# Attention probabilities of the wide units: the transposed unit leaves PSUM through two engines, one bank each

## The chip, the cores and the metric

One NeuronCore of a Trainium2 chip runs the whole kernel. The metric is the device time of one execution in microseconds, the median of three runs; lower is better.

## The reference

A decoder trunk of two layers over 256 tokens of width 1024, in float32. Only the attention matters here:

```python
# layer 0: for each of 8 heads, the selected-block and the window branch of one
# attention, and a top-k branch (dsa) of another; layer 1: 16 heads of "fox"
s = q @ k.T * HEAD_DIM ** -0.5 (+ bias)     # causal
p = softmax(where(valid, s, -1e30))
o = p @ v
...
x = layer_norm(ALPHA * x + concat(o) @ w_o)
x = layer_norm(ALPHA * x + moe(x))          # 64 experts, top 8, plus a shared one
```

## The kernel before

Each engine has an instruction stream of its own, written out by hand, and semaphores order them. Layer 0 projects the inputs, runs the attention, the output projection (`wo`), a layer norm, the router and the shared expert, and then 32 steps of two experts each. Layer 1 does the same with another attention. SyncE issues the weight loads into a ring of four slots, each load when the matmuls that read the slot's old contents are done.

**The attention pipeline.** The work is cut into units of four heads by 128 queries. Layer 0 has 12 units and layer 1 has 8. In the first half of each list (t = 0: units 0 to 5, and 0 to 3) a head has 128 keys, in the second half (t = 1: units 6 to 11, and 4 to 7) it has 256. A unit of t = 1 is called wide: its transposed probabilities are 128x1024 and fill PSUM banks 4 and 5; those of a t = 0 unit are 128x512 and fill bank 4. All engines run over the same iterations u, and in iteration u

- TensorE: the scores of unit u (L598, in layer 1 also L602) and its mask (L614) into PSUM banks 0 to 3; then the transposes of unit u-3 (L634) into banks 4 and 5; then the product with the values (L668, in layer 1 L663) of unit u-4. When there are no scores left, iterations 12 to 15 (8 to 11 in layer 1) have eight matmuls of `wo` (L703) behind the rest.
- VectorE (DVE): the row maxima of unit u (L1523), the copy of unit u-3 from PSUM into `pT` (L1533, one instruction over both banks), then the coefficients of unit u-1 (L1545, L1550) and the scaling of its last head (L1555). Now and then it copies a finished output bank into `xT` (L1560).
- ScalarE (ACT): four exponentials with row sums of unit u (L1214), now and then an output bank into `xT` (L1228).
- GpSimd (POOL): scales three heads of unit u-1 (L531) once its coefficients are there.

Each engine executes its stream in order. There is one pair of banks for the transposes, so TensorE waits before the transposes of unit v for the copy of unit v-1:

```python
pe.wait_ge(sem("sc_scaled"), B + v + 1)
pe.wait_ge(sem("sc_scaled_last"), B + v + 1)
if v:
    pe.wait_ge(sem("pT_copied"), B + v)
```

`B` is 0 in layer 0 and 12 in layer 1. `UNITS` is the list of units, each (kind, t, g); `pT` has two halves, for even and odd units. `PIECE` is 512, one bank.

Of the kernel before, what the change touches and what calls it, by code (L numbers as in the profile page):

```python
# [7 lines left out]
ACT = mybir.ActivationFunctionType  # L8
# [48 lines left out]
PIECE = 512  # L57
# [52 lines left out]
def build_trunk(nc, a, out):  # L110
    with ExitStack() as ctx:
# [253 lines left out]
        def n_keys(t):  # L365
            return (t + 1) * P

        def unit_slots(g):

            return [4 * g + 2 * j + parity for parity in range(2) for j in range(2)]  # L370
# [181 lines left out]
        def _(pe):  # L552
# [22 lines left out]
            def attention(L):  # L575
# [3 lines left out]
                for u in range(U + 4):  # L579
                    if L == 0 and u == 2:  # L580

                        pe.wait_ge(sem("roped"), 5)
                        transpose_pairs(5)
                    if L == 0 and u == 3:
                        pe.wait_ge(sem("qkT_copied"), 6)
                    if u < U:
                        what, t, g = units[u]
                        K = n_keys(t)
                        if u >= 2:

                            pe.wait_ge(sem("sc_exp"), B + u - 1)
                        for j in range(2):

                            heads = [(unit_slots(g)[2 * half + j], slice(HD * half, HD * half + HD),
                                      ps[:, 2 * (u % 2) + half, j * K:(j + 1) * K]) for half in range(2)]
                            for h, r, o in heads:
                                q0, k0, _ = BRANCH.get(what, (0, 2 * 8 + 2 * (h // 2), None))
                                ins = pe.matmul(o, qkT[r, (q0 + h) // 2 if what != "fox" else h // 2, t * P:(t + 1) * P],  # L598
                                                qkT[r, k0 // 2, 0:K], start=j == 0, stop=False, skip_group_check=True)
                            if what == "fox":  # L600
                                for h, r, o in heads:
                                    ins = pe.matmul(o, aug_q[r, h // 2, t * P:(t + 1) * P], aug_k[r, 0:K],  # L602
                                                    start=False, stop=False, skip_group_check=True)
                        if u == 0 and L == 0:
                            pe.wait_ge(sem("causal_cast"), 1)
                        if what == "dsa":
                            pe.wait_ge(sem("selected"), t + 1)
                        for half in range(2):
                            o = ps[:, 2 * (u % 2) + half, 0:2 * K].rearrange("p (s k) -> p s k", s=2)
                            if what == "dsa":  # L610
                                mask, n = selected_bf[t], K
                            else:
                                mask, n = causal_bf, P
                            ins = pe.matmul(o[:, :, K - n:K], ident_bf, mask.unsqueeze(1).to_broadcast([P, 2, n]),  # L614
                                            start=False, stop=True, skip_group_check=True)
                        ins.then_inc(sem("sc_mm"), 1)
                    if L == 0 and u == 2:

                        pe.wait_ge(sem("cmp_p"), NT)
                        for tt in range(NT):  # L620
                            ins = pe.transpose(ps[:, 6, tt * P:(tt + 1) * P], cmp_s[:, tt, :], ident)
                        ins.then_inc(sem("cmp_pT"), 1)
                    if 3 <= u < U + 3:
                        v = u - 3
                        t = units[v][1]

                        pe.wait_ge(sem("sc_scaled"), B + v + 1)
                        pe.wait_ge(sem("sc_scaled_last"), B + v + 1)
                        if v:
                            pe.wait_ge(sem("pT_copied"), B + v)  # L630
                        for s in range(4):
                            for c in range(t + 1):
                                b = s * (t + 1) + c
                                ins = pe.transpose(ps[:, 4 + b // 4, (b % 4) * P:(b % 4 + 1) * P],  # L634
                                                   scores[:, v % 4, s * n_keys(t) + c * P:s * n_keys(t) + (c + 1) * P],
                                                   ident)
                        ins.then_inc(sem("unit_tp"), 1)
                    if L == 0 and u in CMP_STEP:

                        tt = CMP_STEP.index(u)  # L640
                        pe.wait_ge(sem("cmp_pT_copied"), 1)
                        for j in range(4):
                            pe.matmul(ps[:, 7, j * P:(j + 1) * P], v_bd[:, j * P:(j + 1) * P], small_pT[:, tt, :],
                                      start=False, stop=False, skip_group_check=True)
                    if u >= 4:
                        v = u - 4
                        what, t, g = units[v]
                        bank = out_bank(what, g)
                        pe.wait_ge(sem("pT_copied"), B + v + 1)
                        if t and (bank, t) not in opened:  # L650

                            n = [e[0:2] for e in OUTS[L]].index((bank, 0))
                            pe.wait_ge(sem("oT_act" if n % 2 == 0 else "oT_dve"), 2 * L + n // 2 + 1)
                        probs = pT[:, v % 2, 0:4 * (t + 1) * P].rearrange("p (s c k) -> p s c k", s=4, c=t + 1)
                        first = (bank, t) not in opened
                        opened.add((bank, t))
                        c0 = (2 * g % 4) * P
                        for c in range(t + 1):
                            if what == "fox":
                                for j in range(2):  # L660
                                    for half in range(2):
                                        h = unit_slots(g)[2 * half + j]
                                        ins = pe.matmul(ps[half * HD:(half + 1) * HD, bank, c0 + j * P:c0 + (j + 1) * P],  # L663
                                                        v_fox[:, c, h * HD:(h + 1) * HD], probs[:, 2 * half + j, c, :],
                                                        start=first and c == 0 and j == 0, stop=c == t, skip_group_check=True)
                            else:
                                for half in range(2):
                                    ins = pe.matmul(ps[half * HD:(half + 1) * HD, bank, c0:c0 + 2 * P],  # L668
                                                    proj[:, c, BRANCH[what][2]:BRANCH[what][2] + HD],
                                                    probs[:, 2 * half:2 * half + 2, c, :],  # L670
                                                    start=first and c == 0, stop=c == t, skip_group_check=True)
                        ins.then_inc(sem("pv_mm"), 1)
                    if u >= U:

                        i = u - U
                        if i == 0:
                            pe.wait_ge(sem("oT_act"), 2 * L + 1)
                            pe.wait_ge(sem("oT_dve"), 2 * L + 1)
                            pe.wait_ge(sem("sc_exp"), B + U)
                        wo(L, 0, i // 2, range(4 * (i % 2), 4 * (i % 2) + 4))  # L680
# [508 lines left out]
        def _(act):  # L1189
# [12 lines left out]
            def attention(L):  # L1202
                units = UNITS[L % 2]
                U, B = len(units), FIRST_UNIT[L]
                for u in range(U + 4):
                    if u < U:
# [6 lines left out]
                        for s in range(4):  # L1213
# [2 lines left out]
                                                 ACT.Exp, bias=neg_max[:, u % 2, s:s + 1],  # L1216
                                                 accum_out=denom[:, u % 8, s:s + 1])
                        ins.then_inc(sem("sc_exp"), 1)
                    if L == 0 and u == 1:
                        copy_pairs(5, SCALE)  # L1220
                    if L == 0 and u == 2:
# [242 lines left out]
        def _(dve):  # L1464
# [48 lines left out]
            def attention(L):  # L1513
                units = UNITS[L % 2]
                U, B = len(units), FIRST_UNIT[L]
                for u in range(U + 4):
# [9 lines left out]
                    if 3 <= u < U + 3:  # L1526
                        v = u - 3
                        dve.wait_ge(sem("unit_tp"), B + v + 1)
                        if v >= 2:

                            dve.wait_ge(sem("pv_mm"), B + v - 1)
                        n = 4 * n_keys(units[v][1])
                        dve.tensor_copy(pT[:, v % 2, 0:n], ps[:, 4:6, :].rearrange("p b n -> p (b n)")[:, 0:n])\  # L1533
                           .then_inc(sem("pT_copied"), 1)
                    if L == 0 and u == 0:
                        cmp_probs()
                    if 1 <= u <= U:
# [422 lines left out]
```

## Time and profile before

| | |
|---|---|
| median of 3 runs | 1404.83 us (1401.96 to 1406.74) |
| the profiled execution, its own time | 1406.07 us |
| its span, first to last instruction | 1403.8 us |
| mean granted TensorE clock | 0.993 of full speed |
| attention of layer 0 | about 88 to 142 us of the span |
| experts of layer 0 | about 188 to 662 us |
| attention of layer 1 | about 797 to 842 us |
| experts of layer 1 | about 884 to 1362 us |

The times in the rows below are microseconds from the start of the span; 2.3 us of the profiled execution lie outside it. A row of a timeline has the start, the duration, the engine, the line and the operation with its output and input, and in brackets how long the engine stood idle before it and what ended that.

### The profile page before, as it was taken

The page shows a single profiled execution, that of the slowest core. Times are in us where ns is not written, and L with a number is a line of the kernel's source. Part 1 is how long each engine was busy: PE and PEld are TensorE (multiplying, and loading weights), DVE is VectorE, ACT ScalarE, POOL GpSimd, SP SyncE. Part 2 cuts the span into 40 slices and gives each one's busy share as a digit, 9 for nine tenths or more (in the row PEclk, how much of TensorE's full clock was granted, in tenths as well). Part 3 has the DMA queues.
Part 4 walks back from the last instruction along what each step waited for, and adds up shares of the span by engine and source line. Part 5 has one row for each costly group of instructions (what it writes and reads, how often), then busy time and mean ns, then how long its engine had stood idle before and what let it go on. Part 6 is the DMA issues. An engine that isn't in the chain of part 4 may idle for free.

```text
span 1403.8 us, 21736 instructions
## 1 busy us (share of the span) xinstructions
PE 1377.4 (98%) x8662; PEld 848.6 (60%) x8662; DVE 509.4 (36%) x825; ACT 340.0 (24%) x870; POOL 118.3 (8%) x155
## 2 busy tenths in 40 slices
PE   9989999999999999999999999999999999999998
PEld 4555666666566566665488467666656656666553
DVE  1565642332333323234501246232323323333354
ACT  1233232222222222222210222322222222222212
POOL 1555210000000000000100133000000000000000
PEclk9979999999999999999999999999999999999999
DMA  9720459999999999999564504699999999999981
GB/s 303 285 91 1 180 209 411 422 421 420 421 421 420 421 420 421 420 420 383 174 235 149 212 0 180 267 421 421 421 420 421 421 421 421 421 421 420 420 346 60
DMA packets 81110, 461.88 MB, mean 329 GB/s; under 512 B 9216, under 2 KB 9440, under 8 KB 30848
## 3 DMA queue, kind: packets, MB, share of 16 engines
q1 hardware_dynamic: 78432, 452.07, 79.2%
q0 software_dynamic: 2592, 8.53, 2.0%
q8 instruction: 71, 1.16, 0.3%
q14 instruction: 15, 0.12, 0.0%
HBM read 459.52 MB, written 1.05 MB: 328 GB/s over the span
## 4 chain that ended last, share of the span: by engine, by line
PE 88%; DVE 5%; DMA 4%; POOL 1%; issue 1%; ACT 1%; SPq 0%; DVEq 0%; POOLq 0%
PE ps L1025 30%; PE ps L1053 15%; PE ps L1071 9%; PE ps L988 8%; PE ps L703 4%; PE ps L1183 4%; DMA ring<-in_exp_w_dram 3%; PE ps L884 3%; PE ps L805 2%; PE ps L901 2%; PE ps L1035 1%; PE ps L869 1%; PE ps L723 1%; PE ps L598 1%; PE ps L634 1%
## 5 line engine op out<-in xcount | busy, mean ns | idle before, releaser
L1053 PE MATMUL ps<-ring,qkT 128*64 128x512 f32 x1024 | 233.8, 598 | 0.0
L1025 PE MATMUL ps<-ring,proj 128*64 128x256 f32 x2048 | 227.0, 379 | 2.2 <-DMA ring<-in_exp_w_dram 2.2
L1025 PEld LDWEIGHTS ps<-ring,proj 128*64 128x64 f32 x2048 | 147.6, 137 | 88.6 <-issue 20.2
L1822 DVE TENSOR_TENSOR o_tok<-ps,o_tok 128x1024 f32<-128x1024 f32 x124 | 151.8, 1224 | 90.9 <-PE ps L1071 89.9
L1828 DVE TENSOR_TENSOR y_lo<-ps,y_hi 128x1024 fp32r<-128x1024 f32 x62 | 76.0, 1225 | 226.7 <-ACT y_hi L1393 226.7
L1814 DVE SCALAR_TENSOR_TENSOR roped<-roped,rows,ps 128x256 f32<-128x256 f32 x64 | 30.7, 480 | 307.2 <-ACT roped L1366 299.3
L1053 PEld LDWEIGHTS ps<-ring,qkT 128*64 128x64 f32 x1024 | 67.8, 136 | 111.8 <-issue 110.4
L1025 PE MATMUL ps<-ring,pT 128*64 128x256 f32 x1024 | 121.5, 379 | 0.0
L1025 PE MATMUL ps<-ring,gb_row 128*64 128x256 f32 x1024 | 121.4, 379 | 0.0
L1393 ACT ACTIVATE y_hi<-ps 128x1024 fp32r<-128x1024 f32 x62 | 63.5, 1024 | 216.0 <-PE ps L1053 216.0
L1071 PE MATMUL ps<-y_hi,selT 128*128 128x512 f32 x248 | 109.2, 440 | 0.0
L1025 PEld LDWEIGHTS ps<-ring,pT 128*64 128x64 f32 x1024 | 73.4, 137 | 49.5 <-issue 17.1
L1366 ACT ACTIVATE roped<-ps 128x256 f32<-128x256 f32 x64 | 24.6, 385 | 319.1 <-PE ps L1025 319.1
L988 PE MATMUL ps<-sel,x_hi 128*128 128x512 f32 x256 | 101.6, 397 | 0.0
L988 PE MATMUL ps<-sel,x_lo 128*128 128x512 f32 x256 | 100.7, 394 | 0.0
L1071 PE MATMUL ps<-y_lo,selT 128*128 128x512 f32 x248 | 98.5, 397 | 0.0
L1025 PEld LDWEIGHTS ps<-ring,gb_row 128*64 128x64 f32 x1024 | 73.6, 137 | 37.0
L497 POOL DMA_DIRECT2D gb_row<-in_ln_g_dram x4 | 2.6, 650 | 829.9 <-PE ps L1025 821.7
L1071 PEld LDWEIGHTS ps<-y_hi,selT 128*128 128x128 f32 x248 | 47.2, 190 | 29.1 <-issue 23.8
L1372 ACT ACTIVATE qkT<-ps 128x256 f32<-128x256 f32 x64 | 24.6, 384 | 163.1 <-PE ps L1035 163.1
L531 POOL TENSOR_SCALAR roped<-roped,rows 128x128 f32<-128x128 f32 (+1 forms) x60 | 47.0, 798 | 123.5 <-DVE rows L1545 113.7
L703 PE MATMUL ps<-ring,xT 128*128 128x512 f32 x128 | 57.4, 599 | 0.0
(275 smaller groups left out, 1507.4 us busy)
## 6 DMA issues: line engine op xcount, KB each, us to landing
ring<-in_exp_w_dram SPq DMA_DIRECT2D x384, 1024.0 KB, 12.9
ring<-in_od_w_in_dram SPq DMA_DIRECT2D x6, 2048.0 KB, 9.4
ring<-in_ple_w_gate_dram SPq DMA_DIRECT2D x4, 2048.0 KB, 13.1
ring<-in_ev_w_in_dram SPq DMA_DIRECT2D x3, 2048.0 KB, 16.8
ring<-in_sh_w_dram SPq DMA_DIRECT2D x6, 1024.0 KB, 7.8
ring<-in_ev_w_o_dram SPq DMA_DIRECT2D x2, 2048.0 KB, 10.5
ring<-in_od_w_o_dram SPq DMA_DIRECT2D x2, 2048.0 KB, 8.1
gb_row<-in_ln_g_dram POOLq DMA_DIRECT2D x4, 512.0 KB, 8.3
```

Source lines behind the costliest of these rows:

```text
L531: ins = pool.tensor_scalar(part, part, coef[:, v % 4, s:s + 1], None, ALU.mult)
L703: ins = pe.matmul(ps[:, 2 * t + n, :], xT[:, c, t * P:(t + 1) * P], w[:, c, :], start=(c == 0), stop=(c == DC - 1))
L884: ins = pe.matmul(ps[:, (2 * j + half) % 4, b * SEQ:(b + 1) * SEQ], w[:, c, (2 * half + b) * P:(2 * half + b + 1) * P], xT[:, c, :], start ...
L988: ins = pe.matmul(ps[:, bank + c, :], part[:, t, (2 * j + c) * P:(2 * j + c + 1) * P], sel[:, t, :], start=(t == 0 and part is x_hi), stop ...
L1025: ins = pe.matmul(ps[b * SLOTS:(b + 1) * SLOTS, 2, w * FE:(w + 1) * FE], xe(odd, c)[:, u * P + b * SLOTS:u * P + (b + 1) * SLOTS], views[b ...
L1053: ins = pe.matmul(ps[b * SLOTS:(b + 1) * SLOTS, 4 + half, :], hT[:, f, b * SLOTS:(b + 1) * SLOTS], views[b][:, f, half * PIECE:(half + 1) ...
L1071: ins = pe.matmul(ps[:, bank + half, :], selT[:, par, t * P:(t + 1) * P], part[:, half * PIECE:(half + 1) * PIECE], start=(part is y_hi), ...
L1183: ins = pe.matmul(ps[:, 2 * t + n, :], xT[:, c, t * P:(t + 1) * P], w[:, c, :], start=(c == 0), stop=(c == DC - 1))
L1393: act.activation(y_hi[:, :], ps[:, 4:6, :], ACT.Copy).then_inc(sem("y_high"), 1)
L1814: dve.scalar_tensor_tensor(h_exp, h_silu, slot_gate[:, par:par + 1], ps[:, 2, FE:2 * FE], ALU.mult, ALU.mult)\
L1822: dve.tensor_tensor(y_acc[:, t, :], ps[:, bank:bank + 2, :].rearrange("p b n -> p (b n)"), y_acc[:, t, :], ALU.add)\
L1828: dve.tensor_tensor(y_lo[:, :], ps[:, 4:6, :].rearrange("p b n -> p (b n)"), y_hi[:, :], ALU.subtract)\
```

## The change

For the wide units alone the copy into `pT` becomes two instructions: VectorE copies the first bank (bank 4), ScalarE the second (bank 5), with a semaphore of its own, `pT_copied_act`. ScalarE's instruction stands in iteration u, behind the exponentials of unit u. TensorE waits for both semaphores, before the transposes of the next unit and before the product with the values; `wide(L, v)` counts the wide units ahead of unit v. VectorE's copy is 128x512 for every unit.

```diff
+        def wide(L, v):
+            return sum(u[1] for u in UNITS[0]) * L + sum(u[1] for u in UNITS[L][:v])
...
                         if v:
                             pe.wait_ge(sem("pT_copied"), B + v)
+                            pe.wait_ge(sem("pT_copied_act"), wide(L, v))
...
                         pe.wait_ge(sem("pT_copied"), B + v + 1)
+                        pe.wait_ge(sem("pT_copied_act"), wide(L, v + 1))
...
                         ins.then_inc(sem("sc_exp"), 1)
+                    if 3 <= u < U + 3 and units[u - 3][1] == 1:
+                        v = u - 3
+                        act.wait_ge(sem("unit_tp"), B + v + 1)
+                        if v >= 2:
+                            act.wait_ge(sem("pv_mm"), B + v - 1)
+                        act.activation(pT[:, v % 2, PIECE:2 * PIECE], ps[:, 5, :], ACT.Copy).then_inc(sem("pT_copied_act"), 1)
...
-                        n = 4 * n_keys(units[v][1])
-                        dve.tensor_copy(pT[:, v % 2, 0:n], ps[:, 4:6, :].rearrange("p b n -> p (b n)")[:, 0:n])\
-                           .then_inc(sem("pT_copied"), 1)
+                        dve.tensor_copy(pT[:, v % 2, 0:PIECE], ps[:, 4, :]).then_inc(sem("pT_copied"), 1)
```

## Rows read from the trace of the kernel before

**Rows 1.** The page: busy time, share of the span and instructions of each engine.

```profile
PE 1377.4 (98%) x8662; PEld 848.6 (60%) x8662; DVE 509.4 (36%) x825; ACT 340.0 (24%) x870; POOL 118.3 (8%) x155
```

**Rows 2.** Busy time by stretch: both attentions; last columns are clock, DMA share, GB/s.

```profile
88.40:142.00 53.60, 50.82 (x317) 31.57 (x317) 33.39 (x70) 24.50 (x102) 28.90 (x38) 0.92 0.09 38
789.00:841.00 52.00, 48.72 (x339) 30.34 (x338) 21.47 (x37) 17.84 (x69) 18.96 (x24) 1.00 0.21 83
```

**Rows 3.** Two lines of the kernel: instructions, ns min/median/max, shapes.

```profile
L1533 DVE COPY pT<-ps x20: 680/954/1225, 98.8 to 831.8; 128x512 f32<-128x512 f32 x10, 128x1024 f32<-128x1024 f32 x10
...
L1228 ACT ACTIVATE xT<-ps x4: 598/603/610, 111.3 to 827.3; 128x512 f32<-128x512 f32 x4
```

**Rows 4.** Timeline of layer 0, iterations 8 to 12.

```profile
109.52 0.47 ACT L1214 ACTIVATE roped<-ps,rows 128x256 f32<-128x256 f32 x1 [1.37 <-DVE rows L1523]
...
111.33 0.61 ACT L1228 ACTIVATE xT<-ps 128x512 f32<-128x512 f32 x1
...
114.65 0.47 ACT L1214 ACTIVATE roped<-ps,rows 128x256 f32<-128x256 f32 x1 [0.79 <-DVE rows L1523]
...
116.52 1.04 PE L634 MATMUL ps<-const,roped 128*128 128x128 f32 x8
...
118.20 0.47 ACT L1214 ACTIVATE roped<-ps,rows 128x256 f32<-128x256 f32 x1 [1.61 <-DVE rows L1523]
...
119.67 2.89 POOL L531 TENSOR_SCALAR roped<-roped,rows 128x256 f32<-128x256 f32 x3 [0.65 <-DVE rows L1550]
...
120.01 1.04 PE L634 MATMUL ps<-const,roped 128*128 128x128 f32 x8
120.21 1.23 DVE L1523 TENSOR_REDUCE rows<-ps 128x4 f32<-128x1024 f32 x1 [0.24 <-PE ps L614]
...
121.35 1.22 DVE L1533 COPY pT<-ps 128x1024 f32<-128x1024 f32 x1
121.47 0.47 ACT L1214 ACTIVATE roped<-ps,rows 128x256 f32<-128x256 f32 x1 [1.34 <-DVE rows L1523]
...
122.71 1.06 PE L634 MATMUL ps<-const,roped 128*128 128x128 f32 x8 [0.65 <-DVE pT L1533]
```

**Rows 5.** Timeline of layer 1, iterations 7 and 8.

```profile
818.27 1.22 DVE L1533 COPY pT<-ps 128x1024 f32<-128x1024 f32 x1
818.39 0.47 ACT L1214 ACTIVATE roped<-ps,rows 128x256 f32<-128x256 f32 x1 [1.34 <-DVE rows L1523]
...
819.63 1.07 PE L634 MATMUL ps<-const,roped 128*128 128x128 f32 x8 [1.08 <-DVE pT L1533]
...
821.65 3.70 PE L703 MATMUL ps<-ring,xT 128*128 128x512 f32 x8
```

**Rows 6.** Experts: a stretch by engine, PE's wait for weights, SyncE's queue in layer 0.

```profile
300.00:400.00 100.00, 100.00 (x688) 61.29 (x686) 32.54 (x35) 23.34 (x57) 0.00 (x0) 1.00 1.01 421
...
PE ps L1025 <- DMA ring<-in_exp_w_dram: 1.6, 1, 1.6
...
151.89 0.33 SPq L381 DMA_DIRECT2D ring<-in_exp_w_dram  x1
...
188.11 0.33 SPq L381 DMA_DIRECT2D ring<-in_exp_w_dram  x1
```

**Rows 7.** TensorE's clock around idle times: two timeline rows, four stretches (clock third from last).

```profile
96.56 0.85 PE L598 MATMUL ps<-qkT 64*128 64x128 f32 x8 [1.76 <-ACT qkT L1235]
...
669.78 6.58 PE L1167 MATMUL ps<-ring,pT 128*128 128x512 f32 x11 [2.88 <-issue]
...
93.00:97.00 4.00, 2.24 (x22) 1.53 (x21) 2.97 (x10) 2.91 (x13) 2.47 (x5) 0.93 0.02 6
97.00:100.00 3.00, 3.00 (x21) 2.16 (x18) 1.78 (x5) 2.46 (x14) 1.16 (x3) 0.50 0.00 0
...
670.00:674.00 4.00, 4.00 (x6) 1.54 (x5) 3.81 (x6) 0.00 (x0) 0.00 (x0) 0.57 0.09 18
...
819.00:821.00 2.00, 1.37 (x14) 1.24 (x16) 1.79 (x5) 1.32 (x6) 1.34 (x2) 1.00 0.00 0
```

## The prediction

> **What bounds the kernel now.** I read the page first, then the busy time by stretch, then the timeline of the two attentions engine by engine. TensorE is busy for 98% of the span [rows 1], so whatever makes it wait is paid in full, and work taken off another engine is worth nothing unless TensorE was waiting for it. In the attentions it is a little less full: idle for 53.60 - 50.82 = 2.8 us of layer 0's stretch and 3.3 us of layer 1's, while DVE is busy for 33.39 and 21.47 us and ACT for 24.50 and 17.84 [rows 2]. What the change touches shows in the idle time ahead of the transposes. TensorE waited for a copy into `pT` twice in the whole trace: 0.65 us at 122.71 [rows 4] and 1.08 us at 819.63 [rows 5], so 1.73 us in all. Before the other wide units' transposes the copy was done in time, or eight `wo` matmuls lay in front of them (3.70 us, as at 821.65 [rows 5]). The most that this change can gain is therefore small, and the question is what its new instruction waits for.
>
> **What it removes.** Ten of the 20 copies are wide: 1.22 us each, against 0.68 us for 128x512 [rows 3, 4]. DVE loses 10 x 0.54 = 5.4 us of work. At the two places above DVE's part would be ready 0.54 us sooner. Elsewhere the time saved on DVE is idle time.
>
> **What it adds on ScalarE.** Ten copies of 128x512 out of PSUM. The same shape by the same engine is in the trace, 598 to 610 ns [rows 3]; I take 0.60 us. ACT is idle for 1.61 and 1.34 us before two of its groups of exponentials [rows 4], so a copy of 0.60 fits there and delays no exponential. That is not the cost. The cost is the place in the queue: in iteration u the copy of unit u-3 stands behind the four exponentials of unit u, and TensorE's next transposes stand behind the copy. From the first exponential of a wide unit until ACT takes the instruction behind them 1.81 us pass (109.52 to 111.33 [rows 4]). From the end of a copy to TensorE's start I take the 0.14 us between DVE's copy (121.35 + 1.22 = 122.57) and the matmul at 122.71 [rows 4]. So the second bank is free for TensorE at the start of the exponentials + 1.81 + 0.60 + 0.14 = + 2.55 us. There are three iterations in which a wide copy meets wide exponentials and no `wo` matmul lies ahead of the next transposes, 9 to 11 in layer 0, and one in layer 1, iteration 7.
>
> *Layer 0, copy of unit 6.* The exponentials of iteration 9 start at 114.65, so bank 5 is free at 117.20. The transposes of unit 7 ran at 116.52, without a wait [rows 4]. TensorE comes 0.68 us late.
>
> *Layer 0, copy of unit 7.* The exponentials of iteration 10 start at 118.20, a little sooner with the shorter DVE copy before them: free at 120.75 or earlier. The transposes of unit 8 come to 120.01 + 0.68 = 120.69 [rows 4]. I take nothing; at most 0.06 us.
>
> *Layer 0, copy of unit 8.* The row maxima of unit 11 wait for TensorE's scores and start at 120.21 now, 120.89 then, and the exponentials behind them at 121.47 + 0.68 = 122.15. Free at 124.70. The transposes of unit 9 ran at 122.71 [rows 4]. TensorE is 1.99 us late, the 0.68 included.
>
> *Layer 1, copy of unit 4.* Exponentials at 818.39, free at 820.94, against 819.63 [rows 5]: 1.31 us late. Here too the old wait for DVE's copy goes and the longer one for ACT's takes its place.
>
> *The last three copies of each layer* have no exponentials ahead of them on ACT, and TensorE has 3.70 us of `wo` after the transposes: nothing.
>
> The four waits that TensorE checks instead of three come 38 times. The transposes at 120.01 stand behind three waits and show no idle time [rows 4], so I take 0. If every new wait ahead of the wide transposes cost the 0.14 us above, it would be 1.4 us; that is the upper end. POOL needs its unit's coefficients, which DVE computes behind its copy; for unit 9 it ended at 119.67 + 2.89 = 122.56 [rows 4], so it is done by the time TensorE starts at 124.70 even if it slips by those 0.68.
>
> The sum of the delays is 1.99 + 1.31 = 3.3 us.
>
> **Is the delay given back later?** In the experts' stage TensorE and the DMA engines are both full (100.00 of 100 us, share 1.01 at 421 GB/s), and once TensorE waits 1.6 us for weights near the end of layer 1 [rows 6]. If the DMA set the pace there, a late TensorE would cost nothing. But the loads are released by TensorE's own matmuls: the second expert's at 151.89 after a `wo` matmul, the fourth's at 188.11 after the shared expert's [rows 6]. They move with it, so I count the delay in full.
>
> **The clock.** A longer idle time can cost more than itself. After 1.76 us of idle before 96.56 the granted clock was 0.50 from 97 to 100, that is 1.2 instead of 2.4 GHz; after 2.88 us before 669.78 it was 0.57 on average from 670 to 674 [rows 7]. After the 1.08 us before 819.63 it stayed at 1.00 [rows 5, 7]. The changed kernel idles for 0.65 + 1.99 - 0.68 = 1.96 us before the transposes of unit 9, and for 1.08 + 1.31 = 2.39 us in layer 1. Both lie between the idle time that was harmless and the one of 2.88 us, and both above the 1.76 us that was followed by a fall. A fall costs (1 - 0.57) x 4 = 1.7 us of full-speed work; some of it hides in start-up times, so I take 1.6. I count one of the two as the likeliest. The sum is then 3.3 + 1.6 = 4.9 us.
>
> The Trainium skill bears on this ("TensorE: Matmul & The Clock Gate", section "What's actually happening"): the throttled state is the default and activity releases it. Taken strictly, both idle times would be followed by a fall, which is the third case below; the rows at 96.56 and 669.78 agree with it.
>
> **The rivals.**
>
> 1. *The delay alone* (no fall): 3.3 us. For it: in all of layer 1's attention the clock stayed at 1.00 through its idle time [rows 2].
> 2. *The delay and two falls*: 3.3 + 3.2 = 6.5 us. For it: both idle times exceed 1.76 us [rows 7].
> 3. *The two copies run side by side*, the other side. If ACT took its copy ahead of the exponentials, or had them done, the copy into `pT` would last 0.68 instead of 1.22 us, and at both places where TensorE waits it would start 0.54 us sooner: -1.1 us, of the 1.73 us that are there. It decides where ACT's part ends no later than 122.57 in layer 0 and 819.49 in layer 1. Against it: ACT's stream is in order, and exponentials start at 121.47 and 818.39, last 1.81 us and so end at 123.28 and 820.20, after those points [rows 4, 5]. This rival would need a pipeline in which maxima, and so exponentials, come some 1.3 us earlier, and nothing here makes them.
> 4. *Swallowed by the experts' stage*: 0. For it the full DMA and the 1.6 us; against it the releases [rows 6].
>
> The Trainium skill speaks for the third rival ("PSUM — Partial Sum Buffer", section "Specifications (TRN2)"): ScalarE and VectorE can read PSUM in parallel at full bandwidth as long as they don't meet in a bank, and here they have a bank each. By that rule the change gains 1.1 us. No row of before shows the two at it together; whether they may is not the obstacle I see, but when ACT comes to it.
>
> **How the numbers follow.** The profiled execution took 1406.07 us of its own, 1.24 us above the median of 1404.83, and the sum of 4.9 us is put on the median: 1409.7 us (1411.0 for an execution like the profiled one). The delay alone gives 1408.1, two falls 1411.3, side by side 1403.7, swallowed 1404.8. Chances: one fall 0.34, two 0.26, none 0.24, side by side 0.08, swallowed 0.08. The range leaves out the last two: from the delay alone less some 2 us of scatter, which three runs of before show, to two falls with the upper end for the waits: 1406.0 to 1412.8. A measurement of this kernel tells a change from none at about 0.3%, 4.2 us. Over it lie two falls and most of one fall (4.9 us, near the edge) and little of the delay alone: 0.50. Faster by as much needs more than the 1.73 us that can be gained, so it could only be scatter: 0.04. Within it: 0.46.
>
> **What would show it.** In the changed kernel's profile DVE's wide copy is gone and 0.68 us stands everywhere; ACT has ten copies of 0.60 us into `pT`, those of units 6, 7, 8 and of layer 1's unit 4 directly behind exponentials. TensorE's idle time before L634 is put down to ACT's `pT`: some 0.7 us before unit 7, 2.0 before unit 9, and 2.4 in layer 1 before unit 5. The `wo` matmuls start 2.0 us later in layer 0, counted from the attention's start. The clock by stretch after 124 and after 820 tells the cases apart. The prediction is wrong if ACT's copy ends before TensorE wants the bank, if the wait shows but the experts' stage starts no later, or if the new waits slow TensorE where it shows no idle time.

## The result and the profile after

| | before | changed |
|---|---|---|
| median, 7 runs each | 1403.32 us (1401.53 to 1406.74) | 1410.19 us (1407.82 to 1414.74) |
| ratio, with its 95% interval | | 1.0047 [1.0032, 1.0062] |
| the profiled execution, its own time (span) | 1406.07 us (1403.8) | 1414.74 us (1412.5) |

The kernel became slower by 0.47%. In a second measurement beside other runs of the kernel before the ratio was 1.0042 [1.0026, 1.0058] (1409.53 us median). The prediction was 1409.7 us, and slower with a chance of 0.50. Single executions far above all others count in no ratio here: 1763 and 8039 us of layer0_only and 4406 us of the kernel before.

The page's first part, the instructions of the two copies, and who waited for ScalarE's, to be read beside [rows 1] and [rows 3]:

```profile
PE 1379.5 (98%) x8662; PEld 850.0 (60%) x8662; DVE 504.3 (36%) x825; ACT 345.4 (24%) x880; POOL 118.1 (8%) x155
```

```profile
L1544 DVE COPY pT<-ps x20: 678/682/692, 99.3 to 840.9; 128x512 f32<-128x512 f32 x20
...
L1230 ACT ACTIVATE pT<-ps x10: 597/598/607, 116.9 to 840.9; 128x512 f32<-128x512 f32 x10
...
who waited for it (us, times):
  PE ps L639: 4.9, 3
```

The wide copy is gone from VectorE, whose work falls by 5.1 us, and ScalarE has ten copies of 598 ns more and works 5.4 us longer. Neither of the two is short of time. The last line is what matters: TensorE's transposes, now L639, wait for ScalarE's copy three times, 4.9 us in all (0.54, 1.97 and 2.40). Before they waited for VectorE's copy twice, 1.73 us in all. These 4.9 us are idle time, and it is by chance that they are as much as the 4.91 us that the change is found to cost below: 1.73 us of them were there before, and a slower clock comes on top.

Layer 0, the timeline beside [rows 4]. This execution is 0.46 us later from the start on (the transposes of unit 6 stand at 113.86 instead of 113.40), and that is to be taken off.

```profile
115.11 0.47 ACT L1220 ACTIVATE roped<-ps,rows 128x256 f32<-128x256 f32 x1 [0.79 <-DVE rows L1535]
...
116.92 0.61 ACT L1230 ACTIVATE pT<-ps 128x512 f32<-128x512 f32 x1
...
117.67 1.06 PE L639 MATMUL ps<-const,roped 128*128 128x128 f32 x8 [0.54 <-ACT pT L1230]
...
121.19 1.04 PE L639 MATMUL ps<-const,roped 128*128 128x128 f32 x8
...
122.53 0.68 DVE L1544 COPY pT<-ps 128x512 f32<-128x512 f32 x1
122.65 0.47 ACT L1220 ACTIVATE roped<-ps,rows 128x256 f32<-128x256 f32 x1 [1.80 <-DVE rows L1535]
...
124.46 0.61 ACT L1230 ACTIVATE pT<-ps 128x512 f32<-128x512 f32 x1
...
125.21 1.06 PE L639 MATMUL ps<-const,roped 128*128 128x128 f32 x8 [1.97 <-ACT pT L1230]
```

Follow unit 8: its transposes end at 122.2, VectorE has copied bank 4 by 123.2, and ScalarE, which has the exponentials of unit 11 ahead of it, begins with bank 5 at 124.46 only. TensorE has run out of work at 123.24 and stands still until 125.21. Less the 0.46 us, the transposes of unit 7 are 117.67 - 116.52 - 0.46 = 0.69 us late and those of unit 9 125.21 - 122.71 - 0.46 = 2.04 us. Those of unit 8 waited for nothing.

Layer 1, beside [rows 5]; here the offset is 6.25 us (the transposes of unit 4 stand at 823.18 instead of 816.93).

```profile
824.64 0.47 ACT L1220 ACTIVATE roped<-ps,rows 128x256 f32<-128x256 f32 x1 [1.34 <-DVE rows L1535]
...
826.45 0.61 ACT L1230 ACTIVATE pT<-ps 128x512 f32<-128x512 f32 x1
827.20 1.32 PE L639 MATMUL ps<-const,roped 128*128 128x128 f32 x8 [2.40 <-ACT pT L1230]
828.44 1.98 PE L669 MATMUL ps<-pT,proj 128*64 128x128 f32 x16
830.35 4.15 PE L709 MATMUL ps<-ring,xT 128*128 128x512 f32 x8
```

The transposes of unit 5 are 827.20 - 819.63 - 6.25 = 1.32 us late. After them the same work takes longer: 1.98 us for 16 matmuls that took 1.09 us in the same place before, 4.15 us for the eight that took 3.70 [rows 5]. The busy time by stretch says why; the clock is the third number from the end:

```profile
828.00:830.00 2.00, 2.00 (x19) 1.67 (x17) 1.13 (x3) 0.60 (x1) 0.84 (x2) 0.50 0.00 0
830.00:832.00 2.00, 2.00 (x7) 0.90 (x6) 0.00 (x0) 0.00 (x0) 2.00 (x3) 0.68 0.04 8
832.00:834.00 2.00, 2.00 (x6) 0.85 (x5) 0.00 (x0) 0.00 (x0) 0.30 (x1) 1.00 0.00 0
```

The granted clock fell from 1.00 to 0.50, that is from 2.4 to 1.2 GHz, behind the 2.40 us in which TensorE did nothing. Behind the 1.97 us of layer 0 it stayed at 1.00 in this execution (from 124 to 130).

The loads of the experts' stage moved along with TensorE, beside the row at 151.89 of [rows 6]: 2.50 us later, the delay of 2.04 and the offset of 0.46. The stage itself took as long as before: from the first to the last matmul on `sel,x_hi` of layer 0 it was 602.70 - 187.52 = 415.18 us before and 605.21 - 190.00 = 415.21 us after, and in all 14 profiles of this study it is 415.2 us in either layer.

```profile
154.39 0.33 SPq L385 DMA_DIRECT2D ring<-in_exp_w_dram  x1
```

**A ruler for the rest.** Whole spans scatter more than this change moves. I measure two stretches of TensorE's timeline in every profile instead: in layer 0 from the transposes of unit 6, which GpSimd releases, to the first expert's first matmul (`sel,x_hi`), and in layer 1 from the first mask matmul (`causal_bf`) to the same. Before they are 187.52 - 113.40 = 74.12 us and 883.58 - 798.41 = 85.17 us, after 190.00 - 113.86 = 76.14 us and 892.73 - 804.67 = 88.06 us: 2.02 and 2.89 us longer, 4.91 us together.

The profiled spans differ by 8.7 us, though. Of the other 3.8 us, 5.41 - 2.88 = 2.5 us are one idle time between the layers, at a matmul for which the trace names no releaser: 2.88 us before [rows 7] and 5.41 us after.

```profile
673.34 9.27 PE L1173 MATMUL ps<-ring,pT 128*128 128x512 f32 x16 [5.41 <-issue]
```

Nothing ties it to the change. Of the 14 profiles of this study four have this idle time above 1 us: the kernel before, two of the changed kernel's four (the other is after_look_2, 5.14 us) and by_bank (5.25 us), which has the shortest stretches of all. Its cause stays open.

### The profile page after: what moved, and what is told of

The parts are those of the page before. It is cut to its first block, busy times and chain, and to the rows that moved or that the text cites. A ratio compares the mean times of both kernels' runs of the same rounds, so it can differ in the third digit from the quotient of the medians.

```text
span 1412.5 us, 21790 instructions
## 1 busy us (share of the span) xinstructions
PE 1379.5 (98%) x8662; PEld 850.0 (60%) x8662; DVE 504.3 (36%) x825; ACT 345.4 (24%) x880; POOL 118.1 (8%) x155
## 4 chain that ended last, share of the span: by engine, by line
PE 86%; DVE 5%; DMA 4%; issue 2%; POOL 1%; ACT 1%; SPq 0%; POOLq 0%; DVEq 0%; ACTq 0%
PE ps L1031 30%; PE ps L1059 15%; PE ps L1077 8%; PE ps L994 8%; PE ps L709 4%; PE ps L1189 4%; DMA ring<-in_exp_w_dram 3%; PE ps L890 3%; PE ps L907 2%; PE ps L811 1%; PE ps L1041 1%; PE ps L875 1%; PE ps L729 1%; PE ps L602 1%; PE ps L639 1%
```

## The experiments

Each kernel was timed against the kernel before on the same chip, in five rounds; after_look and after_look_2 are one execution each. The stretches, from one profile of each kernel:

| kernel | layer 0, us (to before) | layer 1, us (to before) | ratio of times, 95% interval |
|---|---|---|---|
| before | 74.12 | 85.17 | |
| changed | 76.14 (+2.02) | 88.06 (+2.89) | 1.0047 [1.0032, 1.0062] |
| after_again | 76.15 (+2.03) | 87.88 (+2.71) | 1.0042 [1.0026, 1.0058] |
| after_look | 76.15 (+2.03) | 88.08 (+2.91) | |
| after_look_2 | 76.14 (+2.02) | 88.06 (+2.89) | |
| tail_only | 74.22 (+0.10) | 85.31 (+0.14) | 1.0012 [0.9994, 1.0031] |
| layer0_only | 77.73 (+3.61) | 85.28 (+0.11) | 1.0027 [1.0009, 1.0044] |
| layer1_only | 74.21 (+0.09) | 88.04 (+2.87) | 1.0013 [0.9996, 1.0030] |
| extra_waits | 74.20 (+0.08) | 85.26 (+0.09) | 1.0004 [0.9989, 1.0020] |
| keep_clock | 77.59 (+3.47) | 88.35 (+3.18) | 1.0048 [1.0032, 1.0065] |
| keep_clock_2 | 76.16 (+2.04) | 86.48 (+1.31) | 1.0017 [1.0002, 1.0032] |
| act_first | 73.67 (-0.45) | 84.75 (-0.42) | 0.9984 [0.9969, 1.0000] |
| act_first_again | 73.67 (-0.45) | 84.73 (-0.44) | 0.9996 [0.9980, 1.0012] |
| by_bank | 73.42 (-0.70) | 84.33 (-0.84) | 0.9987 [0.9973, 1.0001] |

**Where the divided copy costs: tail_only, layer0_only, layer1_only.** A function says which units are divided, with one of the three lines in each kernel; the rest keep VectorE's whole copy. ScalarE's copy and `wide` go by the same function.

```diff
+        def split(L, v):
+            return UNITS[L][v][1] == 1 and v + 3 >= len(UNITS[L])     # tail_only
+            return UNITS[L][v][1] == 1 and L == 0                      # layer0_only
+            return UNITS[L][v][1] == 1 and L == 1                      # layer1_only
...
+                        n = PIECE if split(L, v) else 4 * n_keys(units[v][1])
```

> The copy is divided between the engines only for the last three wide units of each layer, where ScalarE has no exponentials left ahead of it; the other four wide units keep VectorE's whole copy. Theory (the cost is the place behind the exponentials): six of ten divided copies stay and the time is that of the kernel before, within 1 us; TensorE waits 0.65 and 1.08 us for VectorE's copy as before. Rival (the divided copy itself costs, by PSUM reads of two engines side by side, or by the second semaphore): some 6/10 of the loss stays, about +4 us.

> Divided copies in layer 0 alone. Theory: TensorE comes 2.0 us late there, so +2.0 us, and up to 1.6 us more in the executions in which the clock falls after the idle time before unit 9; layer 1 waits 1.08 us as before. With the measured +6.9 us of the whole change and each layer's part additive, this and the kernel for layer 1 alone add up to it. Rival (an effect outside the attentions, such as a later start of the whole program): +4 us or more in both kernels.

> Divided copies in layer 1 alone. Theory: TensorE comes 1.3 us late, and the clock falls after 2.4 us of idle time in most executions, 1.6 us more: +2.9 us. Rival (the clock has no part): +1.3 us, the same as no change to this measurement.

Six of the ten divided copies cost 0.1 us in each layer (TensorE waits 0.76 and 1.21 us for VectorE's copy instead of 0.65 and 1.08), and the time isn't told apart from before. The four copies with exponentials ahead of them on ScalarE carry the loss. TensorE has `wo` matmuls to do behind the transposes in these six places, so tail_only alone wouldn't show a copy that is slow in itself. The rows do: in the changed kernel both engines begin with unit 5 of layer 1 at the same moment and take no longer than alone, and act_first below gains with the same two copies at the places that count.

```profile
828.55 0.60 ACT L1230 ACTIVATE pT<-ps 128x512 f32<-128x512 f32 x1 [1.50 <-PE ps L639]
828.55 0.69 DVE L1544 COPY pT<-ps 128x512 f32<-128x512 f32 x1 [2.28 <-PE ps L639]
```

Each layer has its own loss: in either kernel the untouched layer is 0.1 us from before. By the times, 0.27% and 0.13%, the two add up to 0.40%, where the changed kernel has 0.47%; the intervals are too wide to say more. layer1_only's time alone doesn't tell its theory from its rival either, its stretch does. In layer 0 alone the stretch grew by 3.61 us where the changed kernel's grows by 2.02. The idle times of TensorE are the same in both (0.54 and 1.97 us); what differs is the clock:

```profile
124.26 1.06 PE L642 MATMUL ps<-const,roped 128*128 128x128 f32 x8 [1.97 <-ACT pT L1233]
```

```profile
124.00:126.00 2.00, 1.74 (x14) 1.77 (x15) 0.64 (x2) 0.71 (x2) 1.32 (x2) 0.90 0.00 0
126.00:128.00 2.00, 2.00 (x12) 1.13 (x10) 0.49 (x3) 0.00 (x0) 1.77 (x2) 0.50 0.00 0
```

**Falls counted: after_again, after_look, after_look_2.** The changed kernel unchanged.

> The changed kernel once more, for the count of clock falls and a second measurement beside the others. Theory: from the first transposes of a wide unit to the first expert 2.0 us more than before in layer 0 and 1.3 us in layer 1, each 1.6 us more if the clock falls; in layer 1 it falls, in layer 0 it may. Time +5 to +6.5 us. Rival (something outside the attentions adds to it): the two stretches account for less than the whole difference of the medians.

> One more profile of the changed kernel, for the count of clock falls: in layer 1 in every profile, in layer 0 in some.

> One more profile of the changed kernel for the count of clock falls: again in layer 1; in layer 0 in one of five so far (with the kernel changed in layer 0 alone).

Behind 2.40 us of idle time in layer 1 the clock fell in five profiles of five (the changed kernel's four and layer1_only's), behind 1.97 us in layer 0 in one of five (layer0_only's). In after_again the clock of layer 1 fell some 0.4 us before TensorE started again, so less of the slow time met work: its stretch is 87.88 us and not 88.06.

**What the fall costs: keep_clock and keep_clock_2.** Matmuls without use fill the idle time, in a bank whose scores have been read and which the output projection starts anew.

```diff
+                        if u == U:
+                            pe.wait_ge(sem("sc_exp"), B + U - 1)
+                            for _ in range(4 + L):          # keep_clock; range(2) in keep_clock_2
+                                pe.matmul(ps[:, 1, :], ident, x_tok[:, 0, 0:PIECE], start=True, stop=True)
```

> The changed kernel, with 4 (layer 0) and 5 (layer 1) matmuls of 128x512 put into a free PSUM bank in front of the waits before unit 9's and unit 5's transposes. They last 0.45 us each, about the idle time there, and their result is overwritten by the output projection. Theory: TensorE still comes 2.0 and 1.3 us late, but it isn't idle, so the clock stays at full speed; the time is +3.3 us instead of +5 to +6.5. Rival (the fall has another cause than the idle time, or costs nothing): the time is that of the changed kernel.

The first attempt was mis-sized. The timeline of before shows 3.70 us for x8 such rows, but each matmul of this type has two rows (two matmuls stand as x4 below), so it takes 0.92 us and not 0.45. Four filled 3.70 us in layer 0 and five 4.56 us in layer 1, and TensorE came late by its own filling; the kernel says only that the clock stayed at 1.00 in both places.

> The changed kernel with two filling matmuls of 128x512 at either place instead of four and five. Each takes 0.92 us, twice what the first attempt took them for, so two last 1.85 us and fit into the idle time of 1.97 and 2.40 us. Theory: TensorE starts the transposes of unit 9 and of layer 1's unit 5 at the same time as in the changed kernel, no clock falls, and the stretch of layer 1 is 1.3 us longer than before, not 2.9. Time +3.3 us. Rival (the fall does not hang on the idle time): the stretch of layer 1 is 2.9 us longer and the clock falls as before.

```profile
816.87 1.98 PE L634 MATMUL ps<-x_tok,const 128*128 128x512 f32 x4
819.34 1.07 PE L643 MATMUL ps<-const,roped 128*128 128x128 f32 x8 [0.49 <-ACT pT L1234]
```

```profile
818.00:824.00 6.00, 5.51 (x32) 2.98 (x32) 1.54 (x4) 1.79 (x6) 5.09 (x6) 1.00 0.01 3
```

With two of them TensorE starts the late transposes when the changed kernel does, but without a fall: layer 0 is 2.04 us longer than before, layer 1 is 1.31 us. The fall costs layer 1 88.06 - 86.48 = 1.58 us (1.40 in after_again), and layer 0, where it comes, 77.73 - 76.15 = 1.58 us; for layer 0 this compares layer0_only with the changed kernel, whose idle times are the same. The ratio of the whole kernel went to 1.0017 [1.0002, 1.0032], 2.4 us where 3.3 was expected.

**The waits themselves: extra_waits.** The kernel before with one more wait at each of the 38 places, on a value reached long before.

```diff
                             pe.wait_ge(sem("pT_copied"), B + v)
+                            pe.wait_ge(sem("sc_coef"), B + v)
...
                         pe.wait_ge(sem("pT_copied"), B + v + 1)
+                        pe.wait_ge(sem("sc_coef"), B + v + 1)
```

> The kernel before, with one more wait of TensorE at each of the 38 places where the change adds one, on a semaphore whose value was reached long before; no copy is divided. Theory: 0 us, the checks are done ahead of the matmuls. Rival (each wait costs): 0.14 us each, +5 us at 38 places, or +1.4 us if it counts only ahead of the wide transposes.

They cost 0.08 and 0.09 us in the stretches, in which 27 of the 38 places lie, and nothing that the times show. It stands where TensorE waits for the copy anyway: before unit 9 it is idle for 0.76 us instead of 0.65, and in layer 1 for 1.18 instead of 1.08. The tenth of a microsecond that tail_only and the untouched layers have is of that size too.

**The same copies in a better place: act_first and by_bank.** ScalarE's copy of unit u-3 moves ahead of the exponentials of unit u. The rest is the changed kernel.

```diff
                 for u in range(U + 4):
+                    if 3 <= u < U + 3 and units[u - 3][1] == 1:
+                        ...
+                        act.activation(pT[:, v % 2, PIECE:2 * PIECE], ps[:, 5, :], ACT.Copy).then_inc(sem("pT_copied_act"), 1)
                     if u < U:
                         ...
-                    if 3 <= u < U + 3 and units[u - 3][1] == 1:
```

> The change, with ScalarE's copy of unit u-3 ahead of the exponentials of unit u instead of behind them. Theory: the copy starts when the transposes end, which is before or about when the exponentials can start, so both halves are ready some 0.6 us earlier than the whole copy of before; TensorE waits about 0.1 us before unit 9 and 0.5 us in layer 1 before unit 5, no clock falls, and the time is 0.5 to 1.2 us under the kernel before. Rival (side-by-side reading of PSUM or ScalarE's share is slow in itself): it stays at +3 us or more, or the exponentials come so late that the scores two units on wait.

> act_first once more, beside by_bank, for its interval: 0.9 us under the kernel before by its two stretches, and no clock fall in either attention behind unit 6. Rival: the first measurement was scatter and it is the same or slower.

```profile
121.54 0.60 ACT L1217 ACTIVATE pT<-ps 128x512 f32<-128x512 f32 x1 [1.07 <-PE ps L639]
121.81 0.68 DVE L1544 COPY pT<-ps 128x512 f32<-128x512 f32 x1
122.03 0.47 ACT L1226 ACTIVATE roped<-ps,rows 128x256 f32<-128x256 f32 x1
...
122.74 1.06 PE L639 MATMUL ps<-const,roped 128*128 128x128 f32 x8 [0.23 <-DVE pT L1544]
```

Beside the changed kernel's rows at 122.53 to 125.21: the two copies run at once, the exponentials follow at 122.03 and TensorE at 122.74. This profile has the same offset as the changed kernel's (unit 6 at 113.86), so against it that is 2.47 us sooner, and 0.43 us sooner than before. One order of two blocks on ScalarE turned +4.9 us of the stretches into -0.87. In layer 1 TensorE still waits, 0.68 us and for VectorE, which computes the row maxima first. by_bank therefore gives ScalarE, which comes first, bank 4 and VectorE bank 5, and TensorE waits for each only ahead of the four transposes into that bank.

```diff
-                        if v:
+                        both = v and units[v - 1][1] == 1
+                        if both:
+                            pe.wait_ge(sem("pT_copied_act"), wide(L, v))
+                        elif v:
                             pe.wait_ge(sem("pT_copied"), B + v)
...
+                                if both and b == 4:
+                                    pe.wait_ge(sem("pT_copied"), B + v)
```

> ScalarE's copy first, as in act_first, and the banks exchanged: ScalarE takes bank 4, VectorE, which comes later since it computes the row maxima first, bank 5; TensorE waits for each bank's copy only ahead of the transposes into that bank. Theory: the 0.68 us of idle time in layer 1 before unit 5 go, and the stretches are 0.4 to 0.8 us (layer 0) and 0.8 to 1.1 us (layer 1) shorter than before; the time is 1.2 to 1.9 us under it. Rival (GpSimd's scaling is the next bound): no gain over act_first.

It has no idle time of TensorE above 0.25 us at either place (0.24 us in layer 1, for GpSimd's scaling), and 0.70 + 0.84 = 1.54 us less than before in the stretches. That is most of what was to be had here, near the 1.73 us for which TensorE waited in the kernel before. By the times neither kernel is clearly told apart from the one before: the three intervals reach from 0.9969 to 1.0012, and 1.54 us are 0.11%.

## Why the prediction was right

- **What bounds.** Right. Ten wide copies left VectorE and nothing came of it; TensorE's waits decided.
- **The place in ScalarE's queue** as the cost, right and shown: tail_only (no exponentials ahead) costs 0.1 us, about what the new waits do, act_first (the order reversed) gains.
- **The terms of the delay.** Before unit 7 0.68 us predicted, 0.69 measured; before unit 8 none, none; before unit 9 1.99 and 2.04; layer 1 1.31 and 1.32. The sum 3.30 and 3.36 us. The 2.55 us from the first exponential to TensorE's start came out as 2.56 at all three places (115.11 to 117.67, 122.65 to 125.21, 824.64 to 827.20).
- **The 38 waits.** Taken as 0, measured as 0.17 us in the two stretches, which hold 27 of them. The 1.4 us of the range's upper end didn't come. (That end adds up to 1412.7 us, not 1412.8.)
- **Given back later?** No. The loads moved with TensorE, and the experts' stage took 415.2 us before and after.
- **The clock.** One fall was the likeliest case, at 1.6 us: one fall is what all four profiles of the changed kernel show, always in layer 1, at 1.58 us in three of them and 1.40 in after_again. That it was one and not two or none is in part luck. The prediction gave it 0.34, didn't say which of the two idle times it would be, and had no row that sets them apart: both lay above the 1.76 us that was followed by a fall in the kernel before, and in layer 0 1.97 us were not, in four of five profiles. Its strict reading of the Trainium skill, by which both idle times would be followed by a fall, doesn't hold here for the same reason.
- **The sum** of 4.9 us is what the stretches show, 4.91. The times say 0.47% (6.6 us, interval 4.5 to 8.7) and 0.42% (5.9 us, 3.6 to 8.1). 4.9 us lie in both intervals, in the lower half of both. Falls in layer 0 in some executions would add to it; whether they make the difference wasn't shown. That the forecast of 1409.7 us came within half a microsecond of the median is luck: it was put on 1404.83 us for the kernel before, and the seven runs have 1403.32.
- **The rival on the other side,** both halves side by side for 1.1 us, was rightly held unlikely for this change. The prediction named two ways to it, the copy ahead of the exponentials or exponentials that are done, and then weighed the second alone (maxima 1.3 us earlier). The first was open all the time: the copy waits for the transposes and the exponentials for the maxima, and the transposes are done first. act_first got 0.87 of the 1.1 us. The rule of the Trainium skill ("PSUM — Partial Sum Buffer", section "Specifications (TRN2)") that ScalarE and VectorE can read side by side from a bank each agrees with the rows: 0.60 and 0.69 us at 828.55 with both at it from the same moment on, against 598 to 610 ns [rows 3] and 0.68 us alone.

## What to carry to other kernels

When a part of an instruction goes to a second engine, what counts is not the time it takes there but what stands ahead of it in that engine's stream at the moment at which it is needed; look that up before the durations. Where two blocks on an in-order engine wait for different things, the one whose input is ready first goes first. An idle time like those here, 2.0 and 2.4 us on TensorE, is to be priced with the clock: one fall added 1.58 us to a delay of 3.36. What the clock costs can be told apart by filling the gap with matmuls.

## What the runs showed that I had not expected

- The length of the idle time alone doesn't say whether the clock falls. act_first's profile has 2.59 us of idle time early in layer 0's attention, longer than the 2.40 us that were followed by a fall five times of five, and the clock stayed up:

```profile
98.11 0.72 PE L602 MATMUL ps<-qkT 64*128 64x128 f32 x8 [2.59 <-ACT qkT L1247]
```

```profile
98.00:100.00 2.00, 1.89 (x22) 1.59 (x22) 0.81 (x2) 1.81 (x11) 1.61 (x3) 1.00 0.00 0
```

  Five profiles have 2.59 or 2.60 us there, and in four the clock stayed up; in keep_clock it fell before the idle time was over. Four others have 1.74 to 1.81 us there (1.76 in the kernel before) and all four show a fall; the last five have 1.15 to 1.42 us and show none. And 1.97 us at one place, before the transposes of unit 9, were followed by a fall in one profile and not in four. So a fall is given a chance, not a threshold.
- The clock also fell where TensorE had hardly been idle: in after_again, layer0_only and layer1_only early in layer 1, with no idle time above 0.7 us in the 50 us ahead of it.

```profile
706.53 1.93 PE L866 MATMUL ps<-ring,xT 128*128 128x16 f32 x16 [0.38 <-ACT xT L1200]
```

```profile
708.00:712.00 4.00, 4.00 (x24) 4.00 (x24) 0.00 (x0) 0.00 (x0) 0.00 (x0) 0.58 1.04 402
```

  These rows are after_again's. From the first matmul on `ring,pT` between the layers to layer 1's first mask matmul it has 799.15 - 667.51 = 131.64 us, and after_look, where the clock stayed at 1.00 there, 796.08 - 666.07 = 130.01: 1.63 us for a fall, near the 1.58. Such falls lie outside the two stretches and add to the scatter of the whole times. One of the changed kernel's four profiles has one. Whether the change makes them more frequent, and whether that is part of the loss beyond 4.9 us, stays open.
- An idle time of 2.9 to 5.4 us between the layers, which no instruction that the profile shows releases, comes and goes from execution to execution and isn't tied to one of these kernels, and it is as large as the change. A comparison of the two profiles by their spans would have put 3.8 us too much to the change, 2.5 of them from there.
